# A two-block transformer on one core: the end of a feed-forward computed one token group at a time

## The reference, cut to what matters

```python
def mod_norm(x, m, i, g):
    return rms_norm(x, g) * (1 + m[:, 3 * i + 1, None]) + m[:, 3 * i, None]
def ffn_sublayer(x, m, i, g, w1, w2):
    return x + HALF_STEP * m[:, 3 * i + 2, None] * swiglu(mod_norm(x, m, i, g), w1, w2)
...
x = ffn_sublayer(x, m, 0, norm_g[l, 0], ffn_w_in[l, 0], ffn_w_out[l, 0])
xc = ffn_sublayer(xc, mc, 0, norm_g[l, 0], ffn_w_in[l, 0], ffn_w_out[l, 0])
h = mod_norm(x, m, 1, norm_g[l, 1])
hc = mod_norm(xc, mc, 1, norm_g[l, 1])
u = h @ w_in[l]
...
x = x + m[:, 5, None] * y
x = ffn_sublayer(x, m, 2, norm_g[l, 2], ffn_w_in[l, 1], ffn_w_out[l, 1])
```

## Time and profile before

| | |
|---|---|
| median of three runs | 2793.67 us |
| the profiled execution, device time | 2793.08 us |
| its span, first to last instruction | 2791.3 us |
| PE busy | 2732.5 us, 98% |
| DVE busy | 2067.5 us, 74% |
| ACT busy | 1215.4 us, 44% |
| POOL busy | 521.7 us, 19% |
| mean granted clock of TensorE | 0.994 of full |

### The profile page before, as it was taken

One profiled execution on the slowest core, in us unless ns is written; L12 is line 12 of the kernel. 1 busy time (PEld: TensorE's weight loads), 2 busy tenths in 40 slices (PEclk: granted clock), 3 DMA queues, 4 the chain that ended last, 5 costly groups with the idle time before them and its releaser, 6 DMA issues.

```text
span 2791.3 us, 40204 instructions
## 1 busy us (share of the span) xinstructions
PE 2732.5 (98%) x15618; PEld 2321.3 (83%) x15618; DVE 2067.5 (74%) x3773; ACT 1215.4 (44%) x2228; POOL 521.7 (19%) x449
## 2 busy tenths in 40 slices
PE   7999999999999999999998999999999999999998
PEld 5888878658888878888896999889999888888887
DVE  6989895578999897565766766755797677777776
ACT  5323233454222342222345545665556444444444
POOL 1111113300111111010122000345898000000000
PEclk9999999999999999999999999999999999999999
DMA  7555543223555545353441566424654566666663
GB/s 290 191 187 192 190 137 112 76 98 112 187 181 201 181 156 189 128 189 124 170 157 54 192 222 209 139 84 153 202 152 123 186 189 191 192 192 192 190 192 125
DMA packets 123262, 462.50 MB, mean 166 GB/s; under 512 B 13505, under 2 KB 26689, under 8 KB 109889
## 3 DMA queue, kind: packets, MB, share of 16 engines
q1 hardware_dynamic: 109248, 359.27, 40.1%
q0 software_dynamic: 13824, 100.67, 9.4%
HBM read 452.93 MB, written 6.95 MB: 165 GB/s over the span
## 4 chain that ended last, share of the span: by engine, by line
PE 90%; DVE 6%; issue 1%; ACT 1%; DMA 1%; POOL 1%; POOLq 0%; DVEq 0%; ACTq 0%
PE bank L283 28%; PE bank L284 27%; PE bank L285 27%; PE bank L2513 2%; DVE extension_ffn L956 1%; DVE weight_lo L182 1%; DVE nmax L1441 1%; DMA extension_ffn<-in_w_mods 1%; PE bank L976 1%; PE bank L977 1%; DVE arena L545 1%; PE bank L509 1%; DVE extension_mixer L1434 0%; POOL weight_lo L235 0%; PE bank L817 0%
## 5 line engine op out<-in xcount | busy, mean ns | idle before, releaser
L175 ACT ACTIVATE weight_hi<-weight_ring 128x512 fp32r<-128x512 f32 x1272 | 798.6, 630 | 1182.6 <-PE bank L285 1181.5
L182 DVE TENSOR_TENSOR weight_lo<-weight_ring,weight_hi 128x512 fp32r<-128x512 f32 x1110 | 839.8, 760 | 423.2 <-ACT weight_hi L175 420.8
L283 PE MATMUL bank<-operand_hi,weight_hi 128*128 128x256 f32 (+1 forms) x3168 | 1045.5, 330 | 9.8 <-DVE operand_lo L1589 3.6
L284 PE MATMUL bank<-operand_lo,weight_hi 128*128 128x256 f32 (+1 forms) x3168 | 1033.3, 326 | 0.0
L285 PE MATMUL bank<-operand_hi,weight_lo 128*128 128x256 f32 (+1 forms) x3168 | 1033.0, 326 | 0.0
L283 PEld LDWEIGHTS bank<-operand_hi,weight_hi 128*128 128x128 f32 x3168 | 602.2, 190 | 78.0 <-issue 14.4
L284 PEld LDWEIGHTS bank<-operand_lo,weight_hi 128*128 128x128 f32 x3168 | 602.5, 190 | 53.2 <-issue 0.5
L285 PEld LDWEIGHTS bank<-operand_hi,weight_lo 128*128 128x128 f32 x3168 | 602.2, 190 | 50.6
L956 DVE SCALAR_TENSOR_TENSOR extension_ffn<-extension_ffn,silu_c 128x512 f32<-128x512 f32 x532 | 388.4, 779 | 1.7
L235 POOL TENSOR_TENSOR weight_lo<-weight_ring,weight_hi 128x512 fp32r<-128x512 f32 x162 | 211.7, 1315 | 395.5 <-ACT weight_hi L175 393.4
L283 PE MATMUL bank<-hidden_hi_ffn,weight_hi 128*128 128x512 f32 (+1 forms) x704 | 256.6, 364 | 3.9 <-DVE arena L1209 3.9
(11 more groups left out here) (282 smaller groups left out, 2545.2 us busy)
## 6 DMA issues: line engine op xcount, KB each, us to landing
weight_ring<-in_ffn SPq DMA_DIRECT2D x272, 512.0 KB, 3.5
weight_ring<-in_experts SPq DMA_DIRECT2D x256, 512.0 KB, 3.5
extension_ffn<-in_w_mods POOLq DMA_DIRECT2D x96, 1024.0 KB, 7.7
weight_ring<-in_w_mix SPq DMA_DIRECT2D x56, 512.0 KB, 3.4
weight_ring<-in_w_second SPq DMA_DIRECT2D x52, 512.0 KB, 3.6
spill<-early_retrieve SPq DMA_DIRECT2D x45, 128.0 KB, 3.9
arena<-spill SPq DMA_DIRECT2D x45, 128.0 KB, 3.5
extension_mixer<-in_rel_bias SPq DMA_DIRECT2D x2, 1536.0 KB, 6.7
```

The costliest lines, as they stand in the source:

```text
L175: nc.scalar.activation(self.hi[:, g % 2, h], self.ring[:, g % NS, h], ACT.Copy).then_inc(self.rounded, 1)
L182: self.nc.vector.tensor_tensor(self.lo[:, g % 2, h], self.ring[:, g % NS, h], self.hi[:, g % 2, h].bitcast(F32), ALU.subtract).then_inc(se ...
L283: nc.tensor.matmul(out, a_hi, b_hi, start=start and n == 0, stop=False)
L284: nc.tensor.matmul(out, a_hi, b_lo, start=False, stop=False)
```

## The change

At joins A, B and C, after a feed-forward, output chunks 6 and 7 and the norm are done one token group at a time. The new class `GroupNorm` replaces `Norm` there (join D keeps `Norm`).

- TensorE does group 0 of chunk 6 into bank 4 and of chunk 7 into bank 5, then the modulation's transposes, then group 1 of both into banks 2 and 3. The norm's sums of group 0 stand behind the first weight half of chunk 6, group 1, and the spreading behind the first weight half of chunk 7, group 1. The last `work.sum` now stands ahead of chunk 6. TensorE now waits there for the adds of chunk 5 (`added.at(r)`), where it waited for those of chunk 4 (`added.at(r - 1)`).
- The first pair of weight units of the next stage is done for group 0 over all eight tiles and then, at A and B, for group 1. The sums of group 1 stand behind tile 2 and its spreading behind tile 4.
- ScalarE and VectorE get orders written out for this. The sums take three tiles (0, 6, 7) instead of two. The gathering covers chunks 1 to 5. `keep_warm` is not used.
- At join D `Norm.square` takes the last tile in one piece of 512 columns instead of two of 256.
- `AddProduct` gets branches for a `GroupNorm` that never run, since its norm stays `Norm`.

The core of the diff ("..." is left out):

```diff
 
@@ -475,14 +473,6 @@
 
     def square(self, act, kt):
         nc, t = self.chip.nc, self.width
-        if self.half_added and kt == KT - 1:
-            lo, hi = self.groups[0]
-            act.wait_ge(self.half_added.sem, self.half_added.at(1))
-            nc.scalar.activation(self.h[:, kt, lo:hi], self.x[:, kt, lo:hi], ACT.Square)
-            lo, hi = self.groups[1]
-            act.wait_ge(self.after.sem, self.after.at(self.first + kt + 1))
-            nc.scalar.activation(self.h[:, kt, lo:hi], self.x[:, kt, lo:hi], ACT.Square).then_inc(self.squared.sem, 1)
-            return
         if self.after:
             act.wait_ge(self.after.sem, self.after.at(self.first + kt + 1))
         nc.scalar.activation(self.h[:, kt, 0:t], self.x[:, kt, 0:t], ACT.Square).then_inc(self.squared.sem, 1)
...
+class GroupNorm(Norm):
+    grouped, parts, splits = True, 2, 2 * KT
+
+    def bank(self, g):
+        return self.chip.bank[(7, 4)[g]]
...
+    def sums(self, pe, g):
+        c, nc = self.chip, self.chip.nc
+        if g == 0:
+            pe.wait_ge(self.gathered.sem, self.gathered.at(KT - 3))
+        pe.wait_ge(self.squared.sem, self.squared.at(KT - 1 + g))
+        for kt in (0, 6, 7):
+            for b in range(2):
+                at = g * S + b * P
+                last = nc.tensor.matmul(self.bank(g)[:, 2 * b:2 * b + 2], self.h[:, kt, at:at + P], c.ones[:, 0:2],
+                                        start=(kt == 0 and b == 0), stop=(kt == KT - 1 and b == 1))
+        last.then_inc(self.summed.sem, 1)
+
+    def root(self, act, g):
+        c = self.chip
+        act.wait_ge(self.summed.sem, self.summed.at(g + 1))
+        c.nc.scalar.activation(c.root4[:, 2 * g:2 * g + 2], self.bank(g)[:, 0:4:2], ACT.Sqrt, bias=c.eps[:, 0:1], scale=1.0 / D)\
+            .then_inc(self.rooted.sem, 1)
+
+    def invert(self, dve, g):
+        c = self.chip
+        dve.wait_ge(self.rooted.sem, self.rooted.at(g + 1))
+        c.nc.vector.reciprocal(c.rstd4[:, 2 * g:2 * g + 2], c.root4[:, 2 * g:2 * g + 2]).then_inc(self.inverted.sem, 1)
+
+    def spread(self, pe, g):
+        c = self.chip
+        pe.wait_ge(self.inverted.sem, self.inverted.at(g + 1))
+        for b in range(2):
+            last = c.nc.tensor.matmul(self.bank(g)[:, b * P:(b + 1) * P], c.rstd4[:, 2 * g + b:2 * g + b + 1].to_broadcast([P, P]),
+                                      c.ident[:, :], start=True, stop=True)
+        last.then_inc(self.rstd_there.sem, 1)
+
+    def scale(self, dve, kt, g):
+        lo, hi = self.groups[g]
+        if kt == 0:
+            dve.wait_ge(self.rstd_there.sem, self.rstd_there.at(g + 1))
+        self.chip.nc.vector.scalar_tensor_tensor(self.h[:, kt, lo:hi], self.x[:, kt, lo:hi], self.gain(kt, g), self.bank(g)[:, 0:S],
+                                                 ALU.mult, ALU.mult).then_inc(self.scaled.sem, 1)
...
+    def end_scalar(self, act, units, k):
+        self.square_group(act, 6, 0)
+        self.square_group(act, 7, 0)
+        units.round(act, 0, k + 1, [0])
+        self.root(act, 0)
+        units.round(act, 0, k + 1, [1])
+        self.square_group(act, 6, 1)
+        units.round(act, 0, k + 2, [0])
+        self.round_one(act, 0, 0)
+        self.round_one(act, 1, 0)
+        self.square_group(act, 7, 1)
+        units.round(act, 0, k + 2, [1])
+
+    def end_vector(self, dve, add, units, k, finish):
+        self.gather(dve, 5)
+        add(6, 0)
+        add(7, 0)
+        if finish:
+            finish()
+        units.subtract(dve, 0, k + 1, [0])
+        self.invert(dve, 0)
+        add(6, 1)
+        units.subtract(dve, 0, k + 1, [1])
         self.scale(dve, 0, 0)
-        for kt in range(KT):
-            if kt + 1 < KT:
-                self.scale(dve, kt + 1, 0)
-            self.split(dve, kt, 0)
+        units.subtract(dve, 0, k + 2, [0])
+        self.scale(dve, 1, 0)
+        self.split(dve, 0, 0)
+        add(7, 1)
+
+    def end_tensor(self, pe, units, k, n, x, outs, done, turn):
+
+        nc = self.chip.nc
+
+        def half(c, i, g):
+            lo, hi = self.groups[g]
+            w_hi, w_lo = units.half(pe, 0, k + c - KT + 1, i)
+            for kt in range(KT // 2 * i, min(KT // 2 * (i + 1), n)):
+                b = slice(kt * P - i * HALF, (kt + 1) * P - i * HALF)
+                a_hi, a_lo = x(kt)
+                last = product(nc, outs[g][c - 6][:, 0:S], [((w_hi[:, b], w_lo[:, b]), (a_hi[:, lo:hi], a_lo[:, lo:hi]))],
+                               start=(kt == 0), stop=(kt == n - 1))
+            return last
+
+        for c in (6, 7):
+            half(c, 0, 0)
+            half(c, 1, 0).then_inc(done.sem, 1)
+        if turn:
+            turn()
+        half(6, 0, 1).then_inc(units.used, 1)
+        self.sums(pe, 0)
+        half(6, 1, 1).then_inc(units.used, 1)
+        half(7, 0, 1).then_inc(units.used, 1)
+        self.spread(pe, 0)
+        half(7, 1, 1).then_inc(units.used, 1)
+
+    def start_scalar(self, act):
+        self.round_one(act, 2, 0)
+        self.round_one(act, 3, 0)
+        self.round_one(act, 4, 0)
+        self.root(act, 1)
+        for kt in range(5, KT):
+            self.round_one(act, kt, 0)
+        if self.splits > KT:
+            for kt in range(KT):
+                self.round_one(act, kt, 1)
+
+    def start_vector(self, dve, units):
+        self.scale(dve, 2, 0)
+        self.split(dve, 1, 0)
+        units.subtract(dve, 0, 1, [1])
+        self.scale(dve, 3, 0)
+        self.split(dve, 2, 0)
+        self.scale(dve, 4, 0)
+        self.split(dve, 3, 0)
+        self.scale(dve, 5, 0)
+        self.split(dve, 4, 0)
+        self.invert(dve, 1)
+        self.scale(dve, 6, 0)
+        self.split(dve, 5, 0)
+        self.scale(dve, 7, 0)
+        self.split(dve, 6, 0)
+        if self.splits > KT:
+            self.scale(dve, 0, 1)
+            self.split(dve, 7, 0)
+            for kt in range(KT):
+                if kt + 1 < KT:
+                    self.scale(dve, kt + 1, 1)
+                self.split(dve, kt, 1)
+        else:
+            self.split(dve, 7, 0)
+
+    def start_tensor(self, pe, units):
+
+        nc, both = self.chip.nc, self.splits // KT
+        for g in range(both):
+            lo, hi = self.groups[g]
+            for kt in range(KT):
+                i = kt // (KT // 2)
+                if kt % (KT // 2) == 0:
+                    w = [units.half(pe, 0, j, i) for j in range(2)]
+                pe.wait_ge(*self.in_there(kt, g))
+                b = slice(kt * P - i * HALF, (kt + 1) * P - i * HALF)
+                for j in range(2):
+                    last = product(nc, self.chip.bank[j][:, lo:hi],
+                                   [((w[j][0][:, b], w[j][1][:, b]), (self.hi[:, kt, lo:hi], self.lo[:, kt, lo:hi]))],
+                                   start=(kt == 0), stop=(kt == KT - 1))
+                    if g == both - 1 and j == 0 and kt % (KT // 2) == KT // 2 - 1:
+                        last.then_inc(units.used, 1)
+                if g == 0 and kt == 2:
+                    self.sums(pe, 1)
+                if g == 0 and kt == 4:
+                    self.spread(pe, 1)
+        last.then_inc(units.used, 2)
...
+    if after and width == T2 and first == 2 * KT and kind is Norm:
+        kind = GroupNorm
...
+                if n0 + nh == FT and self.then.grouped and n == 6:
+                    work.sum(pe, work.n - 1)
+                    pe.wait_ge(self.added.sem, self.added.at(r))
+                    self.then.end_tensor(pe, units, u0 + 2 * nh + n + 1, nh, lambda kt: (self.hid_hi[:, kt, 0:t], self.hid_lo[:, kt, 0:t]),
+                                         (chip.bank[4:6], chip.bank[2:4]), self.group_done, lambda: work.turn(pe, work.n))
+                    break
...
+        def add(c, g):
+            lo, hi = self.norm.groups[g]
+            if g == 0:
+                dve.wait_ge(self.group_done.sem, self.group_done.at(c - 5))
+            else:
+                dve.wait_ge(units.used, units.used_at(FFN_UNITS - KT + c))
+            nc.vector.scalar_tensor_tensor(self.x[:, c, lo:hi], chip.bank[(4, 2)[g] + c - 6][:, 0:S],
+                                           chip.half_gates[self.layer][:, self.which, c, g:g + 1], self.x[:, c, lo:hi],
+                                           ALU.mult, ALU.add).then_inc((self.then.half_added, self.added)[g].sem, 1)
+
+        def finish():
+            work.collect(dve, KT // 4 if self.gate_first else 0, work.n)
+            self.finish(dve)
+

```

More of the change, by code:

```diff
@@ L613, with __init__, in_there @@
+class SplitNorm(GroupNorm):
+    splits = KT
+    def __init__(self, chip, *more):
+        super().__init__(chip, *more)
+        self.context_in = chip.context_in.take(KT)
+    def in_there(self, kt, g):
+        there = (self.split_in, self.context_in)[g]
+        return there.sem, there.at(kt + 1)
 class DoubleNorm(Norm):
@@ L1136, in tensor @@
                     work.sum(pe, d - 1)
-        if work:
+        if work and not self.then.grouped:
```

(17 more changed lines are left out.)

96 lines of the change are left out of this document (60 added, 36 removed).

## The result

The changed kernel takes 2800.51 us (median of nine, 2798.99 to 2802.02), the kernel before 2793.56 beside it (nine, 2789.53 to 2793.75): 1.0028 times as long, 95% interval 1.0020 to 1.0037. The forecast was 2800.1. The profiled execution took 2800.13 us, of which 2798.3 us are the span from first to last instruction.

A forecast was written before the change was run, and what follows sets the result against it. PE, busy 98% of the span, bounds the kernel. A and B +1.95 each, C +1.35, D +0.2, clock +1.0: +6.4 on 2793.08 gives 2799.5; the median, 0.6 higher, 2800.1 us. Range 2793.5 to 2804.5.

The forecast's parts named there:

- The wait: Ahead of chunk 6, TensorE waits for chunk 5's adds: start 4.1 us later at A and B, 1.16 at C.
- The tail: From chunk 6 to the first pair's end: 27.70 us at A and B (gain 2.15 each), 21.57 at C (loss 0.19).
- The matmul: In chunks 6, 7 and the pair: a 256-column matmul takes 0.12 us, against 0.227 for 512 columns.
- Join D: Last tile squared in one piece, so the sums start later: cost 0.2 us, at most 0.3.
- The clock: Granted clock may fall behind the new pause: 0 to 1.3 us a join, 0.5 taken at A and B each, together 1.0.

The follow-up runs named there:

- the later moves: Changed kernel with sum and added wait behind chunk 6's group 0, chunk 4's gathering behind chunk 5's adds, a weight-half subtract behind tile 2's remainder: 2790.53 us.

## Why the prediction was right, and where only its total was

- **The wait: its size right, its cause only in part.** Chunk 6 starts 413.21 - 403.90 = 9.31 us behind chunk 5 instead of 5.24 at A, 9.31 at B, 5.22 instead of 4.08 at C: 4.1, 4.1 and 1.1, as forecast. The prediction puts all of it on the wait for chunk 5's adds. That wait ends last, but without it 2.56 of the 4.07 us at A are still there, since the modulation's sum has moved too and waits for GpSimd. The same two moves in the kernel before give the same 9.3 us.
- **The tail: right from chunk 6 on, but its gain is not the grouping's.** Where no low clock lies in it, it is 27.56 (A) and 27.54 (B) against 27.70, and at C 26.78 - 5.24 = 21.54 against 21.57. The idle time ahead of the first tile is 1.34 (1.48), ahead of tile 2 0.73 (0.98). Against 29.85 that is 2.3 us. Of these, 0.91 is the sum, which left the stretch for the pause, and 0.86 is low clock in the kernel before, as the run with join B as before shows. That leaves an estimate of 0.5 us a join for the grouping itself. With the sum back in the stream and both kernels at full clock, A takes 34.73 grouped and B 34.24 ungrouped: nothing is won. Only the later moves, which bring the joins to 33.45, win 0.8.
- **The matmul.** A 256-column matmul costs 0.12 us in the new stream too. The Trainium skill's "Back-to-back issue gap" (page "TensorE: Matmul & The Clock Gate") gives N / 2.4 + 2.5 ns for an isolated one, an estimate of 0.109 us. The measurement decides.
- **Join D: right,** 3.21 against 3.00.
- **The clock: mis-sized.** The step was "I take 0.5 for each of A and B", because C showed no fall before. Against the full-clock values (36.87 at A and B, 26.78 at C) the changed kernel loses 2.44, 1.92 and 1.52 us, 5.9 in all and 4.7 in the second profile, where 1.0 was forecast, with 1.3 a join as the upper bound. That bound came from a window that begins after the fall. Taken from 421 us on, the kernel before has a mean clock of 0.57 over 4 us, which is 1.7 us lost and not 1.3 (line below). In the changed kernel's first profile it also stays low twice as long at A and B, over a stream of matmuls with no idle time to absorb it. C's loss was forecast as nothing. It stands in both profiles of the changed kernel and not in the run with join B as before, which has the same code at C, so its cause is open.

```profile
421.00:425.00 4.00, 3.97 (x22) 3.73 (x21) 1.63 (x5) 1.03 (x4) 0.00 (x0) 0.57 0.98 372
```

- The Trainium skill's section "HAM oscillation — how this bites in real kernels" on the same page has the array at half rate behind waits between bursts. At A and B the trace agrees, with 0.50 behind the pause in both profiles.
- **Why the total fits all the same: luck, in part.** At full clock, against the profile before, the joins cost 1.77 + 1.78 + 1.32 + 0.21 = 5.1 us more (forecast 5.4). With the low clock A, B and C cost 10.8 more in the first pair of profiles and 8.5 in the second, against 6.25 forecast for them. In the first pair "A to B" gave back 2.8 and the stretches ahead of A and behind C 1.1, so the spans differ by 7.0. In the second pair "A to B" took 2.0 more, and the spans differ by 11.1. The medians of nine differ by 6.95. So the first pair hits the forecast because low clocks elsewhere fell out in its favour, and the second pair misses it. Whether the same holds for the medians isn't shown, nor is why the clock falls in one execution near 543 us and not in another.

## What to carry to other kernels

Before a wait is moved ahead, read when its signal comes, not whether it was late where it stood: behind half of chunk 6 the same sum and wait cost little. Look for a second instruction that moved with it, here the sum. A pause that delays a dense stream by some 4 us can cost another 1.2 to 2.4 us in the granted clock, as here at A and B. Products put into the pause held the clock up behind it and won nothing in the total. Compare two stretches at the same granted clock before a gain is called the change's. Price the order on the engines beside (here one subtract and one rounding, moved by a few instructions, started tile 2 0.9 us earlier). Take two profiles before a difference of 3 us between distant stretches is called an effect.

## What was not expected of the hardware

- A VectorE subtract of 128x512 takes 2.16 us while GpSimd subtracts 128x1024, and 0.68 once GpSimd's is cut to 8 columns; at the same place nothing else changed.
- Two profiles of one kernel differ by 3.0 us over 570 us of the same instructions (569.19 and 572.22), while the 341.3 us from B to C agree within 0.04 in all versions. The stretch of 570 us has low granted clocks in it, a different number in different executions; the stretch from B to C has none in any.
- At B of the changed kernel the granted clock fell to 0.50 at 1019.6 us. TensorE had been idle for 2.48 us and had just begun the sum.
